# Down weights of the experts loaded two neighbouring rows to a partition, by halves of the partitions

## The reference, cut to what matters

```
def swiglu(h, w_gate, w_up, w_down):
    return (jax.nn.silu(h @ w_gate) * (h @ w_up)) @ w_down

moe_w_gate, moe_w_up: (1, 8, 1024, 2816)      moe_w_down: (1, 8, 2816, 1024)
```

## Time and profile before

| | |
|---|---|
| three timed runs | 1641.03, 1644.91, 1644.87 us, median 1644.87 |
| profiled execution | 1643.27 us |
| its span, first to last instruction | 1641.4 us |
| its mean granted TensorE clock | 0.972 |
| TensorE busy | 92% (matmul), 80% (weight loads) |
| VectorE, ScalarE busy | 68%, 59% |
| HBM read | 382.85 MB |

### The profile page before, as it was taken

The page is one execution under the profiler, slowest core; times in us unless marked ns, Lnnn a source line. Parts: engine busy times, 40 slices in busy tenths (PEclk is TensorE's granted clock), DMA queues, the critical chain, the costliest instruction groups (busy, mean ns, idle before and its releaser), DMA issues.

```text
span 1641.4 us, 22961 instructions
## 1 busy us (share of the span) xinstructions
PE 1509.3 (92%) x9177; PEld 1307.6 (80%) x9177; DVE 1109.4 (68%) x1068; ACT 964.2 (59%) x1114; POOL 147.1 (9%) x133
## 2 busy tenths in 40 slices
PE   6999988999979999869999998989998899999986
PEld 6979978999979799769997676666766799866664
DVE  4766545444456565466677887878888676788886
ACT  5466435433354664444455786868878444478776
POOL 6200000000042000010001001020200200100200
PEclk9999998999999999979999999999999999999998
DMA  9327524555632375224767998999999667689993
GB/s 313 113 95 249 175 73 141 185 186 179 192 115 92 95 253 182 94 86 155 250 215 263 343 386 311 380 342 357 382 333 375 228 224 254 234 300 380 357 373 142
DMA packets 224148, 385.74 MB, mean 235 GB/s; under 512 B 11925, under 2 KB 114681, under 8 KB 223881
## 3 DMA queue, kind: packets, MB, share of 16 engines
q1 hardware_dynamic: 223072, 382.12, 67.4%
q0 software_dynamic: 512, 0.74, 0.2%
q10 hardware_dynamic: 424, 1.08, 0.2%
HBM read 382.85 MB, written 1.05 MB: 234 GB/s over the span
## 4 chain that ended last, share of the span: by engine, by line
PE 73%; DVE 13%; ACT 10%; issue 4%; DMA 1%; ACTq 0%; SPq 0%; DVEq 0%
PE banks L1670 12%; PE banks L1671 12%; PE banks L1672 12%; PE banks L1668 9%; DVE w_low L1184 8%; PE banks L1669 7%; PE banks L1982 6%; ACT w_high L754 5%; PE banks L1984 5%; PE banks L1918 2%; PE banks L1926 2%; PE banks L1877 2%; PE banks L1863 1%; DVE after_heads L1462 1%; ACT rows L754 1%
## 5 line engine op out<-in xcount | busy, mean ns | idle before, releaser
L1184 DVE TENSOR_TENSOR w_low<-raw,w_high 128x2048 fp32r<-128x2048 f32 x357 | 808.2, 2293 | 287.6 <-ACT w_high L754 278.3
L754 ACT ACTIVATE w_high<-raw 128x2048 fp32r<-128x2048 f32 x357 | 679.6, 1915 | 281.0 <-PE banks L1984 108.4
L1668 PE MATMUL banks<-w_high,rows 128*128 128x512 f32 (+1 forms) x576 | 226.1, 399 | 27.1 <-DVE w_low L1184 19.7
L1670 PE MATMUL banks<-rows,w_high 128*128 128x256 f32 x832 | 239.0, 287 | 11.9 <-DVE rows L1185 8.3
L1671 PE MATMUL banks<-rows,w_high 128*128 128x256 f32 x832 | 238.2, 286 | 0.0
L1672 PE MATMUL banks<-rows,w_low 128*128 128x256 f32 x832 | 238.1, 286 | 0.0
L1669 PE MATMUL banks<-w_low,rows 128*128 128x512 f32 (+1 forms) x576 | 214.4, 379 | 0.0
L1982 PE MATMUL banks<-rows,w_high 128*128 128x320 f32 x704 | 189.3, 313 | 9.2 <-issue 9.2
L1984 PE MATMUL banks<-rows,w_low 128*128 128x256 f32 x704 | 187.2, 282 | 1.8 <-issue 1.8
L1670 PEld LDWEIGHTS banks<-rows,w_high 128*128 128x128 f32 x832 | 162.6, 195 | 13.9 <-issue 13.4
L1671 PEld LDWEIGHTS banks<-rows,w_high 128*128 128x128 f32 x832 | 162.7, 196 | 0.4
(11 more groups left out here) (202 smaller groups left out, 2044.2 us busy)
## 6 DMA issues: line engine op xcount, KB each, us to landing
raw<-in_moe_w_gate_dram SPq DMA_DIRECT2D x176, 512.0 KB, 5.7
raw<-in_moe_w_up_dram SPq DMA_DIRECT2D x176, 512.0 KB, 5.5
raw<-in_moe_w_down_dram SPq DMA_DIRECT2D x176, 512.0 KB, 5.5
raw<-in_w_in_dram SPq DMA_DIRECT2D x40, 512.0 KB, 6.0
raw<-in_xa_wkv_dram SPq DMA_DIRECT2D x32, 512.0 KB, 8.8
raw<-in_dense_w_gate_dram SPq DMA_DIRECT2D x22, 512.0 KB, 4.4
raw<-in_dense_w_up_dram SPq DMA_DIRECT2D x22, 512.0 KB, 4.8
raw<-in_dense_w_down_dram SPq DMA_DIRECT2D x22, 512.0 KB, 4.0
```

What stands on the lines that cost most here:

```text
L754: return act.activation(out_, in_, ACT.Copy, scale=scale)
L1184: return dve.tensor_tensor(out_, in_, plain(high), ALU.subtract)
L1668: pe.matmul(dst, stay[0], move[0], start=start, stop=False, skip_group_check=True)
L1670: pe.matmul(dst, stay[0], move[0], start=start, stop=False, skip_group_check=True)
```

## The change

In `wide_down` the rows are assigned in pairs: partition p of a piece holds the rows `2p` and `2p + 1`, next to each other in memory, as one run of 8 KB. The two DMAs of a piece are no longer split by t but by partitions: the first loads partitions 0 to 63, the second 64 to 127, each 512 KB as before, now 64 runs of 8 KB in place of 128 runs of 4 KB. So that the hidden columns follow in the same order, block j of 128 hidden columns is no longer `j * 128` and the 127 after it: `hidden_columns(j)` takes every second column, starting at `(j // 2) * 256 + j % 2`. It is used where `turn` reads `inner` and where `wide_columns` reads `w_high` and `w_low`, both times as the stationary operand. The number of instructions, of DMAs and of bytes is the same. The dense layer's `down` (line 591) is not changed.

```diff
+        def hidden_columns(j):
+
+            start = j // FPS * FFC + j % FPS
+            return slice(start, start + FFC - FPS + 1, FPS)
+
...
                     dst = view(raw[:, c % RAW, :], 0, FPS, D)
-                    src = a["moe_w_down"][0, e, at:at + FFC, :].rearrange("(t p) n -> p t n", p=P)
-                    load(c, 0, [(dst[:, t, :], src[:, t, :]) for t in range(FPS)])
+                    src = a["moe_w_down"][0, e, at:at + FFC, :].rearrange("(p t) n -> p t n", t=FPS)
+                    load(c, 0, [(dst[h:h + HALF_BLOCK, :, :], src[h:h + HALF_BLOCK, :, :]) for h in (0, HALF_BLOCK)])
...
-                            ins = pe.matmul(dst[:, j, b * P:(b + 1) * P], inner[:, b, j * P:(j + 1) * P],
+                            ins = pe.matmul(dst[:, j, b * P:(b + 1) * P], inner[:, b, hidden_columns(j)],
                                             twice if stacked(b) else ident, start=True, stop=True)
...
-                            dst, cols = banks[:, bank_wide(half, s, j), :], slice(j * P, (j + 1) * P)
+                            dst, cols = banks[:, bank_wide(half, s, j), :], hidden_columns(j)
```

## The result

The changed kernel takes 1842.7 us in the median of four runs (1841.2 to 1844.1) against 1644.9 (1641.0 to 1646.7): a ratio of 1.1215, interval 1.1201 to 1.1230, 198 us slower. The forecast was 1742 with a range up to 1790: the direction was right, the size about half of it.

What follows compares the result with a forecast made beforehand. Small experts have three resources nearly full, loads on time but DMA engines 97% busy; halved down loads would make loads the bound. Profiled 1643.3 + 98 = 1741, given as 1742 for the median of runs, range 1642 to 1790.

Steps and rivals of the forecast that it cites:

- The halved rate: Down loads: if engines meet at a half's entrances, a DMA takes twice as long, 56.6 us per expert, not 28.3.
- What I named as deciding: Down loads: the main step is wrong if a stretch with only them still moves 400 GB/s at a share of 1.
- The other signs: Small experts 110 to 123 us at 280 to 315 GB/s, later down landings, copies waiting for DMAs; wide experts, weight loads unchanged.
- Three quarters of the penalty: Down loads: 21.2 us of added DMA time per expert, since engines sharing an entrance partly miss each other.
- my own sum: Small experts: DMA time 95.1 plus 21.2 us exceeds 97.75 by 18.6; six make 111.6, less 14 for loads in hand: +98.
- the depth: Loads about 6 to 7 us ahead, used up once on entering each of two runs of small experts: -14 us.
- the term for half of the partitions: Down loads: each DMA writing 64 partitions costs between nothing and 28.3 us of DMA time per expert; gain excluded.
- every case I had: Halves share entrances, 1742 (0.59); no limit by partition, 1645 (0.24); fewer runs faster, 1633 (0.10); strided weight loads slower, 1772 (0.07).
- The clock: TensorE: the top of the range, 1790, includes some loss of clock when it idles.
- Longer runs: Down loads: 64 runs of 8 KB for 128 of 4 KB, taken as no gain; other bound 6.8% of down's time.
- Strided operands: Weight loads of every second column, wide experts and turning: taken as nothing, upper bound +127 us in the wide experts.
- A reading of the earlier trace: From slice 22 on, DMA share 9 tenths at 311 to 386 GB/s, except slices 31 to 34, 6 or 7 tenths.

Runs made afterwards that it cites:

- wide-only: Changed kernel with down by halves only in the two wide experts, over all partitions in the six small ones: 1648.6 us.
- The loads and splits: Separate kernel of loads, ScalarE's copy and VectorE's remainder, without TensorE: 20.79 us per step with down by halves against 16.07 over all partitions, six buffers.
- Two-ahead: Changed kernel in which SyncE, before asking for an expert's piece, also waits until the piece two before has landed on all 16 engines: 1776.5 us.
- by rows: Changed kernel, but each down DMA takes one row of each pair over all 128 partitions, in runs of 4 KB: 1649.2 us.
- the loads alone: Separate kernel of loads only, nothing computed, nine stages cutting pieces differently: 219 to 224 GB/s by halves, 387 to 420 over all or every second partition.

## Why the prediction was wrong, point by point

- **The halved rate held.** A DMA into one half of the partitions runs at 223 in place of 410 GB/s, at a busy share of 1; small experts are load-bound, wide ones hide it (wide-only 1648.6 us). What I named as deciding, that a stretch of down loads alone would no longer move 400, came out: in the changed kernel 1071 to 1081 us moves 213 GB/s at a share of 1.00. The other signs did not: the small experts take 120 to 135 us and not 110 to 123, at 250 to 271 GB/s and not 280 to 315.
- **Three quarters of the penalty** was too mild. The loads and splits give 2.36 us per piece, 26.0 per expert, where I put 21.2 and had 28.3 as the bound. With 26.0 my own sum gives 95.1 + 26.0 - 97.75 = 23.4 per small expert, six of them 140, less 14 for the depth: +126, and +5 for the strides, 1776. Two-ahead takes 1776.5. That they agree so closely is in part luck: the depth gave back less than 14 (the first small experts of the two runs, 119.0 and 114.9 us, are some 1 and 5 below the others), and the others, 119.5 to 121.5, are mostly a little below the 121.1 of the sum.
- **The step that failed** is the upper bound of the term for half of the partitions: "nothing, or 28.3 us of DMA time per expert", twice the time of the down loads as the worst. With all of it the sum gave 1785; the kernel takes 1842.7. I took the DMA engines as one resource with a sum of times. I did write that they don't run in step, but took it as a reason for a discount of a quarter. It is where the rest of the loss comes from: one engine falls behind, a piece is complete 12.5 to 12.9 us after its first landing in place of 2.8 to 3.7, and gate and up loads run late with the down loads (the waits after). Held together by the wait, the engines give back 66 us (1842.7 - 1776.5), outside every case I had.
- **The sum now:** 126 (rate) + 5 (strides) + 66 (out of step) = 197 of 198 us. The 66 is the difference of two measured times; the 126 is worked out and has the luck named above in it.
- **The clock** fell to 0.89 to 0.96, where I expected some loss, but I find no share of it in the 66 us. In the three slow experts ScalarE's copies begin 0.1 to 0.7 us after the last landing of their piece on average (4.9 to 6.7 in the same three before), so the loads are waited for and not TensorE. The 134 us expert has a clock of 0.94, and so have the three of two-ahead, which take 119.5 to 121.5 us from copy to copy.
- **Longer runs:** taken at nothing, and nothing in the kernel; 8 KB over every second partition gives 1647.3 us where 4 KB by rows give 1649.2, and their intervals overlap. In the loads alone it is 420 against 410 GB/s. **Strided operands:** taken at nothing, cost 5 us; that term was too small by itself to matter for the range. My own row had a hint of it that I passed over: 491 ns for the crosswise read against the 477 worked out for a plain one is 3% more, and the weight loads are 3% slower. They are different engines, so it may be chance.
- **A reading of the earlier trace rows** was loose: slices 24 and 35 have a DMA share of 8 tenths, slice 35 moves 300 GB/s, and the last slice is idle for the most part. Nothing in the sum rests on it.

What stays open is why one engine falls behind and why the lag starts in some experts and not in others; how exactly a late engine slows the rest; and how much of its price comes through the six buffers, which are asked for again only after the latest landing. In the loads by themselves it built up within eight steps.

None of the kernels beats the one before. What the change was to bring, one run of 8 KB per partition, is had without the loss of the halves by taking every second partition in a DMA, and is worth nothing measurable in the kernel.

## What to carry to other kernels

When a transfer is split in two, split it so that each DMA still covers partitions of both halves: by rows within a partition, or every second partition. Read the GB/s beside the busy share of the DMA engines, since a share of 1 is compatible with half the rate. And where loads of two kinds are mixed in a queue, don't take the sum of their times alone as the worst case: look also at how far the first and the last landing of a piece are apart, for the last one completes it.

## What the runs showed of the hardware that I had not expected

- Holding a queue back to two pieces in flight made a load-bound kernel 66 us faster (1842.7 to 1776.5), and cost the kernel before nothing (1.0004).
- A weight load that reads every second float32 takes 197 to 199 ns in place of 191 to 193.
- Loads all by halves moved 246 to 249 GB/s in the kernel but 224 by themselves.
- Loads alone, with two of six pieces by halves, went from 20.9 to 24.8 us for six pieces within one stage, while the landings of a piece spread from 2.9 to 13.9 us.
